# Norm, combine, scale, transposes and split of x in one block per site, by tiles; the experts' first loads and first gather moved into the route

## The reference

```python
def first_block(x, ...):
    alpha = (2 * DEPTH) ** 0.25
    for i in range(DEPTH):                      # i = 0: windowed attention, i = 1: latent attention
        y = ...attention of layer i...
        h = layer_norm(alpha * h + y, ln_g[i, 0], ln_b[i, 0])
        y = hier_moe(h, ...)                    # 32 experts in 4 groups, the best 2 per token
        h = layer_norm(alpha * h + y, ln_g[i, 1], ln_b[i, 1])
    return h

def second_block(x, c, ctx, ...):
    for layer in range(DEPTH):
        u = modulate(rmsnorm(x, norm_mix_g[layer]), sh1, sc1) @ w_in[layer]      # and the same for ctx
        ...mixers...; x = x + g1 * (... @ w_out[layer])
        h = modulate(rmsnorm(x, norm_ffn_g[layer]), sh2, sc2)
        x = x + g2 * conv_ffn(h, ...)
        ...the context likewise, in layer 0 only...
    return rmsnorm(x, final_norm_g)
```

## Time and profile before

| | |
|---|---|
| median of 3 runs | 4597.5 us (4597.21 to 4612.19) |
| profiled execution, its own time | 4604.73 us |
| its span, first to last instruction | 4602.9 us, 52977 instructions |
| TensorE matmul, weight load | 3556.0 us (77%), 2904.8 us (63%) |
| VectorE, ScalarE, GpSimd | 2725.2 us (59%), 2114.0 us (46%), 669.8 us (15%) |
| DMA | 643.27 MB, mean 140 GB/s |
| the two costliest groups | L1477 VectorE x392, 881.7 us; L1541 ScalarE x392, 745.2 us |

### The profile page before, as it was taken

One profiled execution on the slowest core, in us unless ns is written; L12 is line 12 of the kernel. 1 busy time (PEld: TensorE's weight loads), 2 busy tenths in 40 slices (PEclk: granted clock), 3 DMA queues, 4 the chain that ended last, 5 costly groups with the idle time before them and its releaser, 6 DMA issues. The chain is left out here.

```text
span 4602.9 us, 52977 instructions
## 1 busy us (share of the span) xinstructions
PE 3556.0 (77%) x17842; PEld 2904.8 (63%) x17842; DVE 2725.2 (59%) x3492; ACT 2114.0 (46%) x2652; POOL 669.8 (15%) x308
## 2 busy tenths in 40 slices
PE   6757999657939999386977676699896867666987
PEld 5746777445737777265867455588785766355865
DVE  4647999755549999675455534444344544445545
ACT  3527999634429999453334202333233433023433
POOL 0015333300025344200001220000000010400000
PEclk9878999878959999798989787899998988778998
DMA  2019999710129999493120001111121220012222
GB/s 94 15 52 367 419 419 411 300 57 19 37 104 415 418 414 411 193 338 125 56 52 6 1 1 46 52 59 64 58 62 44 60 50 1 0 42 74 92 84 80
DMA packets 158172, 643.27 MB, mean 140 GB/s; under 512 B 43482, under 2 KB 55228, under 8 KB 94396
## 3 DMA queue, kind: packets, MB, share of 16 engines
q1 hardware_dynamic: 135116, 617.42, 35.7%
q0 software_dynamic: 10592, 16.81, 1.0%
q10 hardware_dynamic: 12312, 7.10, 0.7%
HBM read 636.82 MB, written 24.35 MB: 144 GB/s over the span
## 5 line engine op out<-in xcount | busy, mean ns | idle before, releaser
L1477 DVE TENSOR_TENSOR w_low<-w_raw,w_high 128x2048 fp32r<-128x2048 f32 x392 | 881.7, 2283 | 61.4 <-ACT w_high L1541 60.5
L1541 ACT CAST w_high<-w_raw 128x2048 fp32r<-128x2048 f32 x392 | 745.2, 1910 | 77.8 <-DMA w_raw<-in_moe_down_dram 40.4
L526 PE MATMUL banks<-w_high,x_high 128*128 128x512 f32 (+3 forms) x1324 | 521.7, 394 | 148.1 <-DVE w_low L447 119.5
L414 ACT CAST w_high<-w_raw 128x512 fp32r<-128x512 f32 (+3 forms) x321 | 190.4, 593 | 698.3 <-PE banks L526 624.2
L526 PE MATMUL banks<-w_low,x_high 128*128 128x512 f32 (+3 forms) x1324 | 505.5, 382 | 0.0
L526 PE MATMUL banks<-w_high,x_low 128*128 128x512 f32 (+3 forms) x1324 | 504.5, 381 | 0.0
L1381 PE MATMUL banks<-w_high,x_split 128*128 128x512 f32 x1024 | 417.8, 408 | 59.8 <-DVE w_low L1477 54.0
L1381 PE MATMUL banks<-w_low,x_split 128*128 128x512 f32 x1024 | 402.6, 393 | 0.0
L526 PEld LDWEIGHTS banks<-w_high,x_high 128*128 128x128 f32 x1324 | 256.3, 194 | 230.5 <-DVE w_low L447 154.4
L2428 PE MATMUL banks<-x_high,w_high 128*128 128x512 f32 (+1 forms) x1056 | 318.4, 355 | 38.1 <-DVE w_low L2468 38.1
L2428 PE MATMUL banks<-x_low,w_high 128*128 128x512 f32 (+1 forms) x1056 | 317.2, 354 | 0.0
(11 more groups left out here) (376 smaller groups left out, 6799.5 us busy)
## 6 DMA issues: line engine op xcount, KB each, us to landing
w_raw<-in_moe_gate_dram SPq DMA_DIRECT2D x132, 1024.0 KB
w_raw<-in_moe_up_dram SPq DMA_DIRECT2D x132, 1024.0 KB, 10.2
w_raw<-in_moe_down_dram SPq DMA_DIRECT2D x132, 1024.0 KB, 10.9
w_raw<-in_w_ada_dram SPq DMA_DIRECT2D x48, 1024.0 KB, 7.3
w_raw<-in_ffn_w_up_dram SPq DMA_DIRECT2D x44, 1024.0 KB
w_raw<-in_ffn_w_down_dram SPq DMA_DIRECT2D x88, 256.0 KB, 2.7
w_raw<-in_w_cols_dram SPq DMA_DIRECT2D x48, 256.0 KB, 2.6
y<-expert_rows SPq DMA_DIRECT2D x8, 1024.0 KB, 10.0
```

Source lines behind the costliest of these rows:

```text
L414: act.copy(WS[0][:, rest % S, 0:w], W[:, rest, 0:w])
L526: ins_ = pe.matmul(psum_of(g), st[:, rest % S, a:b], mv[:, rest % S, x:y], start=start and first + second == 0, stop=stop and first == 1)
L1477: dve.tensor_tensor(WS[1][:, v % LOW, :], WR[:, v % RAW, :], WS[0][:, v % HIGH, :].bitcast(F32), ALU.subtract).then_inc(low, 1)
L1541: act.copy(WS[0][:, v % HIGH, :], WR[:, v % RAW, :]).then_inc(high, 1)
```

## The change

The norm's stages are put in one block, `norm_turn`, that goes by tiles: statistics, square root, scale and row scale of tile t overlap those of its neighbours, and TensorE turns a tile as soon as its rows are scaled. The row scale is on ScalarE for both kinds of norm. The turned x is taken out of PSUM once all tiles of a part (H, or C) are turned, with gain and bias per partition; for a layer norm ScalarE takes out all eight groups and VectorE meanwhile applies gain and bias to the rows of H. At a site with `combine` ScalarE weighs the first of the experts' two rows and VectorE does the rest, ALPHA included. At the feed-forward sites the split of x runs in the same block. Where x is turned after a layer norm, that is two sites before a router and one before the latent layer; the layer norm after the second experts layer has no turn. The four modulated norms are the other sites. The final norm and the latent layer's inner norms keep `norm`.

In the route's block SP issues the first six weight loads after the sentinel's, GpSimd clears the experts' buffers after the sentinel's memset, ScalarE casts units 0 and 1 at its end, VectorE lowers them behind its last memsets and ahead of its wait for the slot list, and GpSimd, after the scatters, waits for the row table and the token list and issues the first gather. `experts` begins with its loop's buffers so filled.

```diff
+    def norm_turn(self, name, tiles, kind, eps, loads=(), combine=None, finish=None, turn=None, beside=None):
+        items = [(k, part) for part in range(len(turn["parts"])) for k in range(KD)] if turn else []
+        by_dve = [finish is None and k % 2 == 0 for k, _ in items]
+        def evac(eng, i):
+            k, part = items[i]
+            a, b, scale, bias = turn["parts"][part]
+            eng.wait_ge(turned, b)
+            dst, src = turn["XT"][:, k, a * P:b * P], self.ps[:, k, 0:(b - a) * P]
+            if by_dve[i]:
+                eng.tensor_scalar(dst, src, scale[:, k:k + 1], bias[:, k:k + 1], ALU.mult, ALU.add).then_inc(out_v, 1)
+            else:
+                eng.activation(dst, src, ACT.Identity, bias=bias[:, k:k + 1], scale=scale[:, k:k + 1]).then_inc(out_a, 1)
...
+            def _(dve):
+                def statistics(t):
+                    src = tiles[t][0]
+                    if combine:
+                        dve.wait_ge(weighted, t + 1)
+                        order.done(dve.scalar_tensor_tensor(out=src, in0=src, scalar=ALPHA, in1=YT[:, t, 0, :],
+                                                            op0=ALU.mult, op1=ALU.add))
+                        order.done(dve.scalar_tensor_tensor(out=src, in0=YT[:, t, 1, :], scalar=weight[:, t, 1:2],
+                                                            in1=src, op0=ALU.mult, op1=ALU.add))
+                    for c in range(2):
+                        ins_ = dve.bn_stats(bn[:, t, 6 * c:6 * c + 6], src[:, c * BANK:(c + 1) * BANK])
+                    order.done(ins_)
...
+                for t in range(n):
+                    statistics(t)
+                    if t >= 1:
+                        scale(t - 1)
+                    if t == 1 and turn and "prepare" in turn:
+                        dve.wait_ge(loaded, 16 * len(loads))
+                        turn["prepare"](dve, order)
+                scale(n - 1)
+                for i in range(len(items)):
+                    if by_dve[i]:
+                        evac(dve, i)
+                    if i >= 2 and "XS" in turn:
+                        lower(i - 2)
...
+                if finish:
+                    dve.wait_ge(loaded, 16 * len(loads))
+                    for t in range(n):
+                        dve.wait_ge(turned if turn else normed, t + 1)
+                        order.done(dve.tensor_tensor(tiles[t][1], tiles[t][1], finish[0], ALU.mult))
+                        order.done(dve.tensor_tensor(tiles[t][1], tiles[t][1], finish[1], ALU.add))
...
+            def _(act):
+                if combine:
+                    weigh(0)
+                for t in range(n):
+                    if combine and t + 1 < n:
+                        weigh(t + 1)
+                    act.wait_ge(stats, t + 1)
+                    act.activation(mv[:, t, 3:4], mv[:, t, 1:2], ACT.Sqrt, bias=eps_t[:, :]).then_inc(roots, 1)
+                    if t >= 1:
+                        normalise(t - 1)
+                normalise(n - 1)
...
+                for i in range(len(items)):
+                    if not by_dve[i]:
+                        evac(act, i)
+                    if i >= 1 and "XS" in turn:
+                        raise_(i - 1)
...
+            def _(pe):
+                for t in range(n):
+                    pe.wait_ge(normed, t + 1)
+                    for k in range(KD):
+                        if part and t == first:
+                            i = items.index((k, part - 1))
+                            pe.wait_ge(out_v if by_dve[i] else out_a, count[i])
+                        ins_ = pe.transpose(self.ps[:, k, (t - first) * P:(t - first + 1) * P],
+                                            tiles[t][1][:, k * P:(k + 1) * P], self.const("ident"))
+                    ins_.then_inc(turned, 1)
```

```diff
 # route, SP
                     sp.dma_start(table.rearrange("(p n) o -> p (n o)", p=P), sentinel[:, :]).then_inc(table_filled, 16)
+                    for v in range(RAW):
+                        self.load_unit(sp, ex, layer, v, 0)
                     sp.wait_ge(scattered, 16 * NT * 2)
 # route, GpSimd
                     pool.memset(sentinel[:, :], SENTINEL).then_inc(filled, 1)
+                    pool.memset(ex["XG"][:, :], 0.0).then_inc(cleared, 1)
+                    ...
+                    pool.wait_ge(cleared, 6)
...
                     pool.wait_ge(scattered, 16 * NT * 2)
+                    pool.wait_ge(rows_out, 16)
+                    pool.wait_ge(tokens_listed, 1)
+                    pool.tensor_copy(ex["gidx"][:, :], cm["tokens"][:, 0:1]).then_inc(ex["listed"], 1)
+                    pool.wait_ge(ex["listed"], 1)
+                    self.gather(pool, ex)
 # route, VectorE
                     order.done(dve.memset(cm["tokens"][:, ROUNDS * PAIRS:], SENTINEL))
+                    for v in range(2):
+                        dve.wait_ge(ex["high"], v + 1)
+                        self.lower_unit(dve, ex, v)
                     dve.wait_ge(listed, 16)
 # route, ScalarE
                     act.activation(e21[:, :], d21[:, :], ACT.Exp).then_inc(exp_2, 1)
+                    for v in range(2):
+                        act.wait_ge(ex["raw_in"][v], 16)
+                        self.raise_unit(act, ex, v)
```

More of the change, by code:

```diff
@@ L1060, in out_projection, with route_logits @@
                                 lambda t: ("residual", ALPHA)) for c in range(2)])
-    def route(self, layer, cm):
+    def route_logits(self, layer, LG):
+        n_log = GROUPS + EXPERTS
+        with ExitStack() as c2:
+            HT = self.sbuf(c2, "hT", [P, KD, T])
+            ring = self.sbuf(c2, "ring", [P, 1, KD * n_log])
+            self.layer_norm(f"r{layer}_ln", layer, 0, HT)
+            w = ring[:, 0, :].rearrange("p (k n) -> p k n", k=KD)
+            self.project(f"r{layer}_logits", ring, [(self.ins["router"][layer], [
+                (LG[:, t, :], [(HT[:, k, t * P:(t + 1) * P], w[:, k, :]) for k in range(KD)],
+                 ("copy", None)) for t in range(NT)])])
@@ L1609, in experts @@
             self.end(sem)
-    def combine(self, layer, cm):
-        nc, H = self.nc, self.H
-        Y = self.Y[layer]
-        with ExitStack() as ctx:
-            sem = self.Sems(self, f"c{layer}")
-            in_sp, step = [sem(f"in{t}") for t in range(NT)], sem("step")
-            YT = self.sbuf(ctx, "y", [P, NT, 2, DM])
-            with nc.Block() as block:
-                @block.sync
-                def _(sp):
-                    for t in range(NT):
-                        sp.dma_start(YT[:, t], Y[t * 2 * P:(t + 1) * 2 * P].rearrange("(p r) d -> p r d", r=2)).then_inc(in_sp[t], 16)
-                @block.vector
-                def _(dve):
-                    order = Order(dve, step)
-                    for t in range(NT):
-                        order.done(dve.tensor_scalar(H[:, t, :], H[:, t, :], ALPHA, None, ALU.mult))
-                        dve.wait_ge(in_sp[t], 16)
-                        for r in range(2):
-                            order.done(dve.scalar_tensor_tensor(out=H[:, t, :], in0=YT[:, t, r, :],
-                                       scalar=cm["weight"][:, t, r:r + 1], in1=H[:, t, :], op0=ALU.mult, op1=ALU.add))
-            self.end(sem)
@@ L1635, in moe_layer @@
-    def moe_layer(self, layer):
-        with ExitStack() as ctx:
-            cm = {"weight": self.sbuf(ctx, "weight", [P, NT, 2]),
-                  "passes": self.sbuf(ctx, "passes", [P, 1], I32),
-                  "slots": self.sbuf(ctx, "slots", [P, 1 + ROUNDS * PAIRS], I32),
-                  "tokens": self.sbuf(ctx, "tokens", [P, ROUNDS * PAIRS + 2], I32)}
-            self.route(layer, cm)
-            self.experts(layer, cm)
-            self.combine(layer, cm)
-        self.layer_norm(f"m{layer}_ln", layer, 1)
@@ L1648, in latent_layer, with moe_layer @@
-    def latent_layer(self):
+    def moe_layer(self, ctx, layer):
+        cm = {"weight": self.sbuf(ctx, "weight", [P, NT, 2]),
+              "passes": self.sbuf(ctx, "passes", [P, 1], I32),
+              "slots": self.sbuf(ctx, "slots", [P, 1 + ROUNDS * PAIRS], I32),
+              "tokens": self.sbuf(ctx, "tokens", [P, ROUNDS * PAIRS + 2], I32)}
+        with ExitStack() as c2:
+            LG = self.sbuf(c2, "logits", [P, NT, GROUPS + EXPERTS])
+            self.route_logits(layer, LG)
+            ex = self.expert_buffers(c2, layer)
+            self.route(layer, cm, LG, ex)
+            self.experts(layer, cm, ex)
+        return self.Y[layer], cm["weight"]
@@ L1851, in modulation, with modulated @@
                                      for layer in range(DEPTH)])
-    def modulated(self, name, layer, which, XT, tiles, beside=None):
+    def modulated(self, name, layer, which, XT, tiles, beside=None, XS=None):
         nc, ins = self.nc, self.ins
@@ L2365, in ffn_layer @@
                     XT = self.sbuf(c3, "xT", [P, KD, ntok])
-                    self.modulated(f"f{layer}", layer, 1, XT, tiles)
```

(3 more changed lines are left out.)

259 lines of the change are left out of this document (171 added, 88 removed).

## The result

The changed kernel takes 4524.67 us in the median of four runs (4520.57 to 4534.8), the kernel before 4598.45 in the four runs beside it (4597.21 to 4612.19): a ratio of 0.9832 with a 95% interval of 0.9813 to 0.9851. The forecast was 4530 with 4508 to 4558. The profiled execution took 4534.8 us with a span of 4533.0, where the one before took 4604.73: 69.9 less.

What follows compares the result with a forecast made beforehand. No engine is full; the experts' loop fills DMA and VectorE together, elsewhere chains run in sequence. Gains 18.2 + 11.6 + 4.8 + 13.5 + 20.6 = 68.7 us, taken from the profiled 4604.73, less 7.2 for the median: 4530, range 4508 to 4558.

Steps and rivals of the forecast that it cites:

- rival A: Routes: nothing blocks the scatters beside VectorE's subtractions, so each route gives 14.4 us; time 4521, chance 0.15.
- The pitch of a tile: Layer norm sites: statistics, small operations, scale and shift take VectorE 1.9 us a tile, 7.75 for four.
- TensorE's end: Layer norm sites: TensorE turns a tile in 1.97 us at clock 0.50 and ends at 11.9.
- The evacuations: Layer norm sites: ScalarE alone takes eight groups out of PSUM, some 0.83 us apart, ending last at 18.6.
- gather's issue against the tokens: Experts' start: issued in the route, the gather comes 6.1 us earlier against the token list.
- issue to the turned tile: Experts' start: with six loads landed before, the gather takes 3.7 us to land in place of 8.73.
- casts of units 0 and 1 done before: Route: casting these units there brings unit 2's cast 3.6 us earlier still.
- subtractions beside the scatters: Route: the second scatter waits for both VectorE subtractions, delaying slot list, tokens and gather by 4.1 us.
- memsets beside VectorE's chain: Start of the route: GpSimd's early memsets cost VectorE's chain 0.3 us.
- B: Norms: handoffs by tile eat the gain, 0.7 us a tile, 22 us less; 4552, chance 0.15.
- C: Experts' loop: a new phase makes gathered tiles late, 3 us a pair; 4625, slower, chance 0.03.
- D: Routes: the prefetch does not carry over, the idle DMA queue sets the loop's end; 5 each, 4540, chance 0.12.

Runs made afterwards that it cites:

- e4: The changed kernel with GpSimd's six memsets of the experts' buffers put behind VectorE's routing weights: 4524.35 us (0.9813).
- e3: The changed kernel with VectorE's subtraction of unit 0 moved ahead of the position copy, that of unit 1 behind the scatters' landing: 4524.46 us (0.9818).
- e5: The changed kernel with the first gather back at the head of the experts' block, the six loads still in the route: 4532.18 us (0.9835).
- e10: e5 with SyncE holding its first two 1 MB loads of the experts' block until the gather has landed: 4518.56 us (0.982).

## Why the prediction was right, and by how much its terms were off

The time came out 5 us under the forecast. The norms went as forecast, with three prices too high. In the routes the chain was the right one, but two waits on it were missing (the memsets', and the block's end behind the gather) and one was priced too dear. So two errors of size have opposite signs: the norms gained 59.5 us where 48.1 were forecast, the routes 13.3 where 20.6 were. That 11 and 7 us mostly cancel is luck. The time alone, 4524.67, lies a little nearer to rival A's 4521 than to the forecast's 4530; it is the rows of the scatters that decide between them.

**Norms, 11 us too little.** The shape held everywhere: TensorE's turns hidden under the statistics, VectorE at its undisturbed 1.22 us. Three prices were too high.

- The pitch of a tile. I allowed 1.9 us. The statistics of the four tiles start at 272.72, 274.17, 275.78 and 277.44, some 1.6 apart, and VectorE's first gain starts at 279.61, 7.1 after the block's start in place of 7.75. The small operations of neighbouring tiles interleave, so no wait across the engines is open. In the modulated norms the pitch is some 1.75.
- TensorE's end. I had every tile cost 1.97 us, at the granted clock's lower level of 1.2 GHz. TensorE had been idle for 7.92 us before its first transpose, after the out projection's matmuls, and starts at that level; but it is then busy without a pause, and the clock rises within the site. Cut over the transposes:

```profile
277.19:280.50 3.31, 3.31 (x16) 3.18 (x16) 3.03 (x11) 2.96 (x5) 0.00 (x0) 0.50 0.05 20
280.50:281.50 1.00, 1.00 (x7) 0.99 (x6) 0.97 (x2) 1.00 (x1) 0.00 (x0) 0.61 0.00 0
281.50:282.90 1.40, 1.37 (x13) 1.14 (x11) 1.37 (x2) 0.10 (x1) 0.00 (x0) 1.00 0.00 0
```

  The last ten or so of the 32 run at 2.4 GHz. All four tiles are turned by 282.87, 10.3 after the start against 11.9. At 1.97 us a tile, by estimate, they would have ended at 285.1: the shorter pitch alone would have left TensorE behind.
- The evacuations: eight at 0.68 us apart (5.46 by 8), where I had 0.83 from the pitch of 0.78 of one instruction. So ScalarE ends at 15.9 (18.6), and VectorE ends the layer norm site at 17.1, not ScalarE. The site gains 10.3 and 10.0 where I had 9.1.

At the sites with the split the same errors add up. The last norm of four tiles:

```profile
4087.15 1.97 PE L1116 MATMUL banks<-consts,xn 128*128 128x128 f32 x8 [11.85 <-ACT xn L1073]
...
4089.42 3.89 PE L1116 MATMUL banks<-consts,xn 128*128 128x128 f32 x24 [0.30 <-ACT xn L1073]
...
4098.69 2.56 DVE L1035 TENSOR_TENSOR x_low<-xT,x_high 128x512 fp32r<-128x512 f32 x4
```

The first tile takes 1.97 us, the three others 3.89 (the clock is 0.50 until 4090.50 and 0.99 from there to 4093.30), and the last is done at 4093.31, 11.2 after the start (12.6 forecast); evacuation and split take 7.9 (9.2): 2.5 us of a term of 2.9 that became 5.4. At combine the rows of the experts landed 6.0 us after the issue, not 5.0, and the pitch was lower, which nearly cancel (12.0 for 11.6).

**Routes, 7 us too much.** Of the 10.3 a route, 6.9 and 6.4 came. By the steps of the working, in the first route:

```
                                       forecast   measured
gather's issue against the tokens        -6.1       -5.7
issue to the turned tile                 -5.0       -2.9
casts of units 0 and 1 done before       -3.6       -3.6
subtractions beside the scatters         +4.1       +2.7
memsets beside VectorE's chain           +0.3       +2.7
sum                                     -10.3       -6.9
```

- The memsets were mis-sized most. The route's step took "0.3" for what they do to VectorE's chain; the small tensor_scalar waits 2.7 us for them, shown by e4. The Trainium skill (SBUF — State Buffer, Who interferes with whom) has the rule that was missing from the working: a tensor_scalar can enter a mode that takes VectorE's shared ports and is then locked out by GpSimd, while a tensor_tensor does not contend with an instruction of GpSimd that only writes. The rows agree on both: 2.85 us for the one, 0.17 for the other. Why the hold outlasts a single memset no run shows.
- The subtractions do hold the scatters up, so the forecast's reading of the earlier trace rows stands, and rival A falls: no scatter beside them took 1 us. The size is 2.7, since the second scatter waits for one subtraction and not for both, and the third for the other. What the prediction took from the Trainium skill (SBUF — State Buffer, Who interferes with whom), that a tensor_tensor leaves the making of descriptors alone, marked there as inferred, would have had the scatters unhindered. The runs are against it: an indirect DMA beside a tensor_tensor takes 2.77 us, and 0.97 in e3, where only the subtractions stand elsewhere. They do not say which part of the DMA is held: a scatter also reads its numbers and addresses from SBUF, and no run separates that from the descriptors.
- The landing. I put the tile 3.7 us after the issue by the fastest row, and the gather did land in that time. The trace has its landing by itself:

```profile
DMA to landing us min/median/max: 3.4/3.4/3.4
```

  But in the route the block's end comes between. The experts' block starts 4.57 us after the issue, 1.17 after the landing, and TensorE's first instruction is at 351.84, behind VectorE's clearing of two banks (350.88 to 351.79): 5.81 in place of 3.7. In the seven profiled executions that have the gather in the route and a traced landing (six kernels, the changed one twice; 14 routes), issue to landing goes from 3.3 to 4.1 us, and the block starts 1.17 us after the landing in every one. In e5 and e10, with the gather out of the route, it starts 1.0 to 1.1 us after the tokens. So the block's end waits for the gather's landing.

**The other rivals.** B: no handoff by tile is open, the norms gained more and not less; out. C: the loop from the cast of unit 2 to its end takes 527.2 and 525.6 us, 527.5 and 527.9 before; the loop got no longer. D: what the cast gained the loop's end gained too, by the same rows; out. e5 shows the weak point that D was near: not the queue's idle end, but the loads that a finished prefetch lets go.

## What to carry to other kernels

In a norm that stands alone on the critical path, start the transposes by tile and leave the elementwise work to one of VectorE and GpSimd; here that was 34 and 10 of 59 us. Before moving work of GpSimd or VectorE into another block, list what the other engine does beside it there, by the kind of instruction: here a memset stopped a tensor_scalar, and a long tensor_tensor an indirect DMA. A DMA issued last on GpSimd in a block is paid for until it lands. And when buffers are filled early, look at which loads this sets free and what latency-bound transfer they then meet.

## What the runs showed of the hardware that I had not expected

- The tile of an indirect gather of 128 rows is turned 3.42 us after the gather's issue with nothing in flight, and 8.32 us with two 1 MB loads issued 0.33 us behind it (e10, e5), though the gather was issued first.
- A block whose last GpSimd instruction is an indirect DMA gives way to the next block 1.17 us after that DMA's landing, in 14 routes of six kernels; with no gather in it, 1.0 us after the last VectorE instruction (e5, e10).
- GpSimd memsets hold a VectorE tensor_scalar of 128x16 for 2.68 us, across several memsets one behind the other, and leave a tensor_tensor of the same size alone.
